# Rotary embedding: most partner rows come by SBUF-to-SBUF transfers from SyncE's queue, not by a TensorE product

## The chip, the cores and the metric
One core of one Trainium2 chip. The metric is the device time of one execution in microseconds; the median of three runs stands for a kernel. A core has TensorE (matmuls), VectorE, ScalarE, GpSimd (POOL) and SyncE, which here only issues transfers. All of them run at once and are ordered by semaphores.

## The reference
Two transformer stacks of two layers each, on 256 tokens with 1024 features in float32; only what matters here:

```python
def apply_rope(x, cos, sin):                 # first stack, heads of 64
    xf = x.reshape(x.shape[:-1] + (HEAD_DIM // 2, 2))
    x0, x1 = xf[..., 0], xf[..., 1]
    return jnp.stack([x0 * cos - x1 * sin, x0 * sin + x1 * cos], axis=-1)
...
        qb = apply_rope(rms_norm(heads(gq, GQA_Q_HEADS), q_gain[l]), cos, sin)
        kb = apply_rope(rms_norm(heads(gk, GQA_KV_HEADS), k_gain[l]), cos, sin)
...
def partial_rope(x, cos, sin):               # second stack, the first 16 of 64
    x1, x2 = x[..., :half], x[..., half:ROPE_DIM]
    r1, r2 = x1 * c - x2 * s, x2 * c + x1 * s
    return jnp.concatenate([r1, r2, x[..., ROPE_DIM:]], axis=-1)
...
    q_c = partial_rope(heads(q_c, N_HEADS_DSA), cos, sin)      # 5 heads
    k_c = partial_rope(k_c[:, :, None, :], cos, sin)[:, :, 0]  # 1, from the compressed keys
    q_i = partial_rope(q_i.reshape(B, S, N_IDX_HEADS, IDX_DIM), cos, sin)
    k_i = partial_rope(rmsnorm(k_i, g_idx_k)[:, :, None, :], cos, sin)[:, :, 0]
```

So in the first stack neighbours (rows 2i and 2i+1 of a head) turn each other, in the second rows i and i+8 of the first 16. Around this stand projections, neighbourhood, grouped-query, forgetting, stick-breaking and sparse attention, and gated feed-forwards.

## The kernel before, in words
Features lie on the 128 partitions, tokens along the free axis, so a chunk of 128 features x 256 tokens holds two heads. Weights come as "pieces" of up to 128 x 2048 (1 MB). SyncE issues them one after another into a ring of four slots: piece n waits until TensorE has begun piece n - 3 (`piece_begun`). ScalarE rounds a piece to its high part `w_hi` (two buffers, L1750), VectorE computes the rest `ring_lo` in the slot (L2267), in halves, and TensorE multiplies high by high, high by low and low by high (L1258 features on the partitions, L1504 tokens on them, L1301 the wide form). Every engine runs its own program in the order in which the host put items into `plan`; there is no scheduler, and VectorE, ScalarE and SyncE never pass over a waiting instruction. An item "inside" another is issued by TensorE among that one's matmuls (`mids`).

A rotation (`rope`) turns 256 tokens of one chunk: TensorE multiplies the chunk with a 128 x 128 matrix of 0, 1 and -1 (`pe_rope`, L1548), which puts each row's partner, with its sign, into a PSUM bank; VectorE multiplies that by the sine table into a scratch (`turned_by`, two halves used in turn), the chunk in place by the cosine table, and adds (`dve_rope`, L2635, L2636, L2638). There are 24: five in each layer of the first stack ("block 1": the key chunk `gk` and four query chunks `gq`), seven in each layer of the second ("block 2": two index-query chunks, two and a half chunks of queries, the index key, the compressed key).

Where they stand. Block 1, layer 0: among attention steps (`att`), which are mixed with gate chunks; a step computes scores (L1572), takes negated maxima (L2668), exponentials (L1989), transposes (L1585) and at times the values' product (L1600). The head norms' factors are spread by L1538 and applied by L2624 (chunks 0 and 1, then 2 and 3, then 4); between them run products for the modulation (L1410), whose weights, `w_mod`, are pieces of the same ring, two at a time (`some(unit, 2)`). Block 1, layer 1: the five are issued among the matmuls of the value product (`tok` of `w_nav`). Block 2: among the chunks of the projection. Two of `w_in`'s chunks lie in a piece; evictions to `arena` scale by the norm (L2496, L2498). `unread` matmuls (L1203) are fillers whose result nobody reads.

SyncE's weight loads are L1188, its first loads L1165 to L1180.

Of the kernel before, what the change touches and what calls it, by code (L numbers as in the profile page):

```python
# [9 lines left out]
ALU = mybir.AluOpType  # L10
# [3 lines left out]
P = 128  # L14
S = 256
D = 1024
KC = D // P
DH = 64
# [37 lines left out]
for _block, _names in (  # L56
        (0, (("ident", P), ("sum_heads", 4 * 32), ("sum_kv", 2 * 32), ("row_sel", 8), ("vec_sel", 64), ("spread", 4 * P))),
        (1, (("rot1", P), ("cos1", S), ("sin1", S), ("na_mask", 2 * S))),
# [10 lines left out]
def constants():  # L69
# [18 lines left out]
    rot = np.zeros((P, P))  # L88
    rot[p[1::2], p[0::2]] = -1
    rot[p[0::2], p[1::2]] = 1  # L90
    put("rot1", rot)
# [5 lines left out]
    put("sin1", np.sin(ang).T[pair])  # L97
# [4 lines left out]
    for h in range(2):  # L102
        for i in range(8):
            a, b = h * DH + i, h * DH + 8 + i
            rot[b, a], rot[a, b] = -1, 1
            cos[a] = cos[b] = np.cos(ang[i])
            sin[a] = sin[b] = np.sin(ang[i])
# [41 lines left out]
class Plan:  # L149

    def __init__(self):
        self.items, self.pieces, self.splits = [], [], []
        self.full, self.taken, self.lin, self.counts = [0] * 8, [0] * 8, 0, {}
        self.in_slot, self.held = [0] * RING, None

# [43 lines left out]
def hybrid_kernel(nc, xt, vec_d, con_d, tables_d, rpb, w, out):  # L199

    with ExitStack() as ctx:
# [130 lines left out]
        setup, silu_c_ready, amp_ready = sem("setup"), sem("silu_c_ready"), sem("amp_ready")  # L332
        x_done, squares, sq_added, rstd_ready = (sem(n) for n in ("x_done", "squares", "squares_added", "rstd_ready"))
# [237 lines left out]

        last_prep, mixed, last_gate = [None], [], [None]
# [57 lines left out]
        def rope(chunks, block, need=(), inside=False, bank=None):  # L630
            return add("rope", block=block, need=need, tb=turned_by if block == 1 else turned_by2, inside=inside,
                       chunks=[(b, a, low, fill(T_BANKS[i % 2] if bank is None else bank) if bank or not inside else linear(), count("rope")) for i, (b, a, low) in enumerate(chunks)])
# [87 lines left out]
        def first_block(l):  # L720
# [18 lines left out]

            def na_pair(i, q0, k0, nk):  # L740
# [37 lines left out]
            if l == 0:  # L778
# [54 lines left out]
                head_spread(hn, 0, 1)  # L833
                some(unit, 2)
# [4 lines left out]
                rope(ropes[:2], 1, need=(hn["spread"][1],))  # L839
# [8 lines left out]
                rope(ropes[2:3], 1, need=(hn["spread"][2],), bank=T_BANKS[1])  # L848
                two_steps(last=False)
                rope(ropes[3:4], 1, need=(hn["spread"][3],))  # L850
                two_steps()
                rope(ropes[4:5], 1, need=(hn["spread"][4],))
# [7 lines left out]
            else:  # L860
# [19 lines left out]
                head_spread(hn, 0, 1)  # L880
                g = attention([dict(na_pair(0, 0, 0, SQ), after=(feats["naq", 0], feats["nak", 0]))])
                att(g)
                run_all(nk[1])
                head_spread(hn, 2, 3)
                vals = values()
                att(g)
                head_spread(hn, 4)
# [4 lines left out]
                among = {4 + 8 * i: rope([r], 1, need=(hn["spread"][i],), inside=True) for i, r in enumerate(ropes)}  # L892
                tok("nav", w["w_nav"][l], 2, SLOT, 512, SQ, nav)
                plan.items[-1]["mids"] = among
                next(vals)
                add("keys_swap", n=plan.counts["rope"] - 4)
# [83 lines left out]
        def second_block(l):  # L980
# [22 lines left out]
            def turned(chunk, bank, *need):  # L1003
                return rope([chunk], 2, need=need, inside=True, bank=T_BANKS[bank])
# [27 lines left out]
            def stick_acc(*hs):  # L1032
                for h in hs:
                    accs.append(fill(T_BANKS[h % 2]))
                    add("stick_acc", h=h, f=accs[-1], n=5 * l + h)

            run_all(chunks(0, fresh=plan.counts["h"], norm=defer()), chunks(1))
            add("y2_pad", after=fc(QI + 1))
            tok(f"vb{l}", w["vb2"][l], 2, 4 * 384, 384, S, vb2, scaled=True, n_out=330)
# [6 lines left out]
            among(t, lambda: {10: [turned((feat2, QI * S, 0), 0, fc(QI))], 18: [turned((feat2, (QI + 1) * S, 0), 1, fc(QI + 1))]})  # L1046
            run_all(t)
            t = chunks(3)
            next(t)
            head_spread(hn, 0, 1)  # L1050
            among(t, lambda: {13: [turned((feat2, 12 * S, 0), 1, fc(12))], 20: [turned((feat2, 13 * S, 0), 0, fc(13))]})
# [5 lines left out]
                              16: [turned((feat2, KX * S, DH), 0, hn["spread"][1])]})  # L1057
            key_turned = plan.counts["rope"]
            add("key_twice", n=key_turned, k=count("key_twice"))
            among(t, lambda: {8: [turned((kc2, 0, 0), 1, kv[0])], 16: [turned((feat2, QX * S, DH), 0, fc(QX))]})  # L1060
            run_all(t)
            among(feat(f"2f{l}", [(0, P, cols(5, 0, P))], [10], S, length=KC * P), lambda: {6: [index(0, 0, 1)], 16: [index(0, 2, 3)]})
            t = chunks(5)
# [100 lines left out]
        def _(sp):  # L1164
# [10 lines left out]

            first_mod(0)
            for p in plan.pieces:
# [5 lines left out]
                for a, n, src in p.srcs:  # L1183
# [4 lines left out]
                    sp.dma_start(dst, src).then_inc(landed[p.slot], 16)  # L1188
            for k in range(4):
# [7 lines left out]
        def _(pe):  # L1197
# [28 lines left out]
            def product(fs, n, groups, fresh=None, need=None, at_col=0, mids={}, more=False, hold=False, odd=None):  # L1226
# [7 lines left out]
                for p, terms in groups:  # L1234
# [6 lines left out]
                    for wpart, part, (at, hi, lo, rows, c), k in order:  # L1241
# [11 lines left out]
                        if at_mm in mids:  # L1253
                            for what, it in mids[at_mm] if isinstance(mids[at_mm], list) else [mids[at_mm]]:
                                dict(sums=pe_sums, spread=pe_spread, att=pe_att, head_spread=pe_head_spread, rope=pe_rope, kvup=pe_kvup,
# [230 lines left out]
            def pe_tok(st):  # L1486
                T, cols, n = st["T"], st["cols"], len(st["pieces"])
                per, at_mm, mids = KC // n, 0, st.get("mids", {})
                for j, p in enumerate(st["pieces"]):
# [3 lines left out]
                    for wt, low in ((w_hi[p.s % 2], False), (ring_lo[p.slot], True)):  # L1493
                        if low:
                            pe.wait_ge(w_lo_ready, 2 * p.s + 2)
                        for t, f in enumerate(st["fs"]):
                            for i in range(per):
                                c, at = j * per + i, i * cols
                                for part in range(1 if low else 2):
                                    if at_mm in mids:  # L1500
                                        pe_rope(mids[at_mm])
                                    at_mm += 1
# [40 lines left out]
            def pe_rope(st):  # L1543
                pe.wait_ge(s_tables, 16 * st["block"])
                taken(*st["need"])
                for buf, at, low, f, _ in st["chunks"]:
                    room(f)
# [697 lines left out]
        def _(dve):  # L2245
# [381 lines left out]
            def dve_rope(st):  # L2627
                b = st["block"]
                dve.wait_ge(s_tables, 16 * b)
                for f in st["need"]:  # L2630
                    taken(f)
# [333 lines left out]
```

## Time and profile before
| | |
|---|---|
| median of 3 runs | 2416.3 us (2415.94 to 2416.79) |
| profiled execution | 2416.34 us |
| its span, first to last instruction | 2414.5 us |
| mean granted TensorE clock | 0.999 of 2.4 GHz |
| TensorE, VectorE, ScalarE, GpSimd busy | 2393.6, 1538.3, 1219.4, 405.0 us |
| transfers | 389.9 MB, 161 GB/s over the span |

A row of a timeline is the start in us from the span's start, the length in us, the engine, the line, the operation, what it writes and reads, its shape and how many were merged; in brackets the idle time before it and what ended it. TensorE's matmul records overlap, so the price of one is read from start to start. SPq is SyncE.

### The profile page before, as it was taken

Reading aid. Unit: us, or ns where it says so; the run is one execution under the profiler, and the core shown is the slowest. Engines: PE = TensorE matmul, PEld = TensorE weight load, DVE = VectorE, ACT = ScalarE, POOL = GpSimd, SP = SyncE. Lnnn points to the kernel's source line nnn. Section 1 sums busy time; section 2 is a strip of 40 time slices with the busy share of each in tenths; the row PEclk is TensorE's granted clock in tenths of the full one; section 3 lists DMA queues with packets and bytes.
Section 4 is the critical chain, followed back from the end, with each engine's and each line's share of the span. In section 5 each row is a group of like instructions: output and inputs, shape, how many; then the busy total and the mean of one; then the engine's idle time right before and its main releaser. Section 6 shows DMA issues by size and latency. Waiting matters only on the chain.

```text
span 2414.5 us, 36498 instructions
## 1 busy us (share of the span) xinstructions
PE 2393.6 (99%) x14216; PEld 2036.5 (84%) x14216; DVE 1538.3 (64%) x2659; ACT 1219.4 (51%) x2268; POOL 405.0 (17%) x388
## 2 busy tenths in 40 slices
PE   8999999999999999999999999999999999999998
PEld 6766689888888877988888899898888889989887
DVE  5335455663455555677677777677767767767775
ACT  4344444322222546565565545665556554566554
POOL 0343322000001335100100100540010010154000
PEclk9999999999999999999999999999999999999999
DMA  6334423453444422455565553355565564436554
GB/s 280 132 114 158 157 88 122 159 169 135 157 165 141 157 89 95 150 192 176 194 212 181 172 184 128 123 193 192 170 208 180 176 195 151 151 112 200 190 175 137
DMA packets 88602, 389.92 MB, mean 161 GB/s; under 512 B 15024, under 2 KB 27600, under 8 KB 58352
## 3 DMA queue, kind: packets, MB, share of 16 engines
q1 hardware_dynamic: 81232, 356.07, 43.4%
q0 software_dynamic: 7200, 31.52, 3.8%
q8 instruction: 114, 1.87, 0.3%
q14 instruction: 56, 0.46, 0.1%
HBM read 386.52 MB, written 1.05 MB: 161 GB/s over the span
## 4 chain that ended last, share of the span: by engine, by line
PE 93%; DVE 3%; ACT 2%; POOL 1%; issue 1%; DMA 0%; DVEq 0%; SPq 0%; POOLq 0%; ACTq 0%
PE ps L1301 42%; PE ps L1258 38%; PE ps L1504 3%; PE ps L1572 2%; PE ps L1585 2%; PE ps L1600 2%; DVE ring_lo L2267 1%; PE ps L1395 1%; ACT logits L1989 1%; ACT w_hi L1750 1%; PE ps L1410 1%; POOL logits L2184 1%; PE ps L1548 1%; DMA x_res<-xt 0%; PE ps L1429 0%
## 5 line engine op out<-in xcount | busy, mean ns | idle before, releaser
L2267 DVE TENSOR_TENSOR ring_lo<-ring,w_hi 128x1024 fp32r<-128x1024 f32 (+4 forms) x708 | 781.8, 1129 | 200.1 <-ACT w_hi L1750 199.0
L1750 ACT ACTIVATE w_hi<-ring 128x1024 fp32r<-128x1024 f32 (+4 forms) x708 | 633.4, 944 | 280.1 <-PE ps L1258 186.7
L1301 PE MATMUL ps<-h_hi,w_hi 128*128 128x512 f32 x2144 | 527.2, 393 | 0.6 <-DVE h_hi L2440 0.3
L1301 PEld LDWEIGHTS ps<-h_hi,w_hi 128*128 128x128 f32 x2144 | 391.3, 188 | 76.6 <-issue 2.5
L1258 PE MATMUL ps<-h_hi,w_hi 128*128 128x256 f32 (+1 forms) x1520 | 410.6, 333 | 2.0 <-ACT arena L1879 1.2
L1258 PE MATMUL ps<-h_lo,w_hi 128*128 128x512 f32 (+1 forms) x976 | 325.5, 351 | 0.0
L1301 PEld LDWEIGHTS ps<-h_hi,ring_lo 128*128 128x128 f32 x2144 | 281.3, 191 | 14.5 <-DVE ring_lo L2267 0.9
L1301 PE MATMUL ps<-h_hi,ring_lo 128*128 128x256 f32 x2144 | 288.2, 282 | 0.0
L1258 PEld LDWEIGHTS ps<-h_hi,w_hi 128*128 128x128 f32 x1520 | 252.3, 190 | 37.6 <-issue 11.2
L1258 PE MATMUL ps<-h_hi,ring_lo 128*128 128x256 f32 (+1 forms) x1248 | 253.3, 338 | 0.3 <-DVE ring_lo L2267 0.3
L2509 DVE TENSOR_TENSOR prob_t<-ps,prob_t 128x256 f32<-128x256 f32 x260 | 109.7, 422 | 196.3 <-ACT prob_t L1902 196.0
L2140 POOL TENSOR_TENSOR logits<-logits 128x256 f32<-128x256 f32 (+1 forms) x65 | 67.6, 1040 | 991.0 <-ACT logits L1771 776.5
L1301 PE MATMUL ps<-hid_both,w_hi 128*128 128x512 f32 x880 | 226.2, 392 | 0.0
L1258 PEld LDWEIGHTS ps<-h_hi,ring_lo 128*128 128x128 f32 x1248 | 200.8, 189 | 28.4 <-issue 2.2
L2184 POOL TENSOR_SCALAR logits<-logits,stat 128x512 f32<-128x512 f32 (+2 forms) x140 | 167.9, 1211 | 261.4 <-DVE stat L2680 261.2
L1902 ACT ACTIVATE prob_t<-ps 128x256 f32<-128x256 f32 x260 | 98.1, 377 | 220.6 <-PE ps L1301 220.3
L1258 PEld LDWEIGHTS ps<-h_lo,w_hi 128*128 128x128 f32 x976 | 182.3, 189 | 23.5 <-DVE h_lo L2440 0.2
L1301 PEld LDWEIGHTS ps<-hid_both,w_hi 128*128 128x128 f32 x880 | 160.8, 188 | 30.9
L1989 ACT ACTIVATE logits<-logits,stat 128x512 f32<-128x512 f32 (+2 forms) x140 | 81.6, 584 | 140.4 <-DVE logits L2668 85.5
L1301 PE MATMUL ps<-hid_both,ring_lo 128*128 128x256 f32 x880 | 133.4, 282 | 0.0
L1301 PEld LDWEIGHTS ps<-hid_both,ring_lo 128*128 128x128 f32 x880 | 122.4, 191 | 5.7
L1928 ACT ACTIVATE prob_t<-prob_t 128x256 f32<-128x256 f32 x110 | 46.0, 418 | 105.3 <-DVE prob_t L2533 93.5
(301 smaller groups left out, 2934.0 us busy)
## 6 DMA issues: line engine op xcount, KB each, us to landing
ring<-w_ffn_in SPq DMA_DIRECT2D x132, 1024.0 KB, 4.9
ring<-w_ffn_out SPq DMA_DIRECT2D x96, 704.0 KB, 4.0
ring<-w_in SPq DMA_DIRECT2D x36, 1024.0 KB, 4.9
ring<-w_w_in SPq DMA_DIRECT2D x26, 1024.0 KB, 5.0
bias_t<-w_mod POOLq DMA_DIRECT2D x24, 1024.0 KB, 5.4
ring<-w_mod SPq DMA_DIRECT2D x16, 1024.0 KB, 6.0
ring<-w_up SPq DMA_DIRECT2D x16, 576.0 KB, 3.8
ring<-w_pab SPq DMA_DIRECT2D x8, 1024.0 KB, 4.9
```

The lines of the kernel that those rows point to most:

```text
L1258: mm = pe.matmul(ps[fs[k].bank][:, at_col:at_col + n], (hi_w if wpart == "hi" else lo_w)[0:rows, at[k]:at[k] + P], hi if part == "hi" else ...
L1301: mm = pe.matmul(ps[f.bank][:, 0:cols], wt[:, at + q * P:at + q * P + P], both[:, 0:cols], start=left[q] == n, stop=left[q] == 1, skip_gro ...
L1504: mm = pe.matmul(ps[f.bank][:, 0:st["n"]], rows, wt[:, at:at + st["n"]], start=c == 0 and part == 0 and not low, stop=c == KC - 1 and low)
L1572: mm = pe.matmul(ps[f.bank][:, s2["at"]:s2["at"] + s2["nk"]], p["q"][a, s2["t"] * P:(s2["t"] + 1) * P], p["k"][a, k0:k0 + s2["nk"]], start ...
L1585: mm = pe.transpose(ps[f.bank][:, c * P:(c + 1) * P], logits[:, o:o + P], ident)
L1750: act.activation(w_hi[q.s % 2][:, h * n:(h + 1) * n], ring[q.slot][:, h * n:(h + 1) * n], ACT.Copy)\
L1902: act.activation(tmp[i][:, S:SQ], ps[f.bank][:, S:SQ], ACT.Copy).then_inc(half_out, 1)
L1989: act.activation(lg, lg, ACT.Exp, scale=-1.0, bias=stat[:, o:o + 1], accum_out=stat[:, 4 + o:5 + o])\
L2140: pool.tensor_tensor(sq_sum[:, o:n], sq_sum[:, o:n], sq[j % 2][:, o:n], ALU.add).then_inc(sq_added, 1)
L2184: pool.tensor_scalar(lg, lg, stat[:, 8 + (a % 2) * 2 + h:9 + (a % 2) * 2 + h], None, ALU.mult)\
L2267: dve.tensor_tensor(ring_lo[q.slot][:, c], ring[q.slot][:, c], plain(w_hi[q.s % 2][:, c]), ALU.subtract)\
L2509: dve.tensor_tensor(tmp[i][:, to:to + S], ps[f.bank][:, 0:S], tmp[i][:, S:SQ], ALU.add).then_inc(psum_taken[f.bank], 1)
```

## The change
Of the 24 rotations 20 lose their product. Instead SyncE copies the chunk's rows, swapped, into the scratch, by transfers from SBUF to SBUF: in block 1 two of 64 rows of every second partition, in block 2 two (or four, for a chunk with two heads) of 8 rows. The sign goes into the sine tables. The four rotations of the index key and of the compressed key keep the product (`product`), with `hroot2` as scratch and a wait for the rotation before. In block 2 the scratch is cleared once, as rows that aren't swapped are multiplied by a sine of 0.

A swap is recorded in `plan.swaps` under a piece's number, and SyncE does it right behind the issue of that piece: two behind the next piece at the time of the call, or more (`later`). SyncE first waits until the chunk is complete, and until the rotation that used the same half of the scratch is done. VectorE's `rope` waits for the landing. In block 1, layer 1, and in block 2 VectorE's rotations take other places in its order.

```diff
+        def swap(chunk, block, need, later=0):
+            buf, at, low = chunk
+            n = count("swap")
+            moves = 2 if block == 1 or low else 4
+            t = dict(buf=buf, at=at, low=low, block=block, need=need, n=n, tb=turned_by if block == 1 else turned_by2,
+                     landed=count(f"swap_landed{n % 2}", 16 * moves))
+            t["before"] = swapped[-2] if n > 2 else None
+            swapped.append(t)
+            plan.swaps.setdefault(len(plan.pieces) + 2 + later, []).append(t)
+            return t
...
+            def swap_rows(t):
+                sp.wait_ge(psum_taken[t["need"].bank], t["need"].taken)
+                if t["before"]:
+                    sp.wait_ge(rope_ready, t["before"]["turned"])
+                src, dst = t["buf"][:, t["at"]:t["at"] + S], t["tb"][:, t["n"] % 2 * S:(t["n"] % 2 + 1) * S]
+                if t["block"] == 1:
+                    for a in range(2):
+                        sp.dma_start(dst[a:P:2, :], src[1 - a:P:2, :]).then_inc(s_swap[t["n"] % 2], 16)
+                    return
+                for h in range(t["low"], P, DH):
+                    for a, b in ((0, 8), (8, 0)):
+                        sp.dma_start(dst[h + a:h + a + 8, :], src[h + b:h + b + 8, :]).then_inc(s_swap[t["n"] % 2], 16)
...
                     sp.dma_start(dst, src).then_inc(landed[p.slot], 16)
+                for t in plan.swaps.get(p.n, ()):
+                    swap_rows(t)
...
# block 1, layer 0
                 head_spread(hn, 0, 1)
+                turned = swaps(0, 1)
...
-                rope(ropes[:2], 1, need=(hn["spread"][1],))
+                rope(*turned)
+                turned = swaps(2, 3, later=2)
                 add("keys_swap", n=1)
...
                 head_spread(hn, 4)
-                rope(ropes[2:3], 1, need=(hn["spread"][2],), bank=T_BANKS[1])
+                rope(turned[0])
+                turned += swaps(4, later=1)
...
# VectorE
             def dve_rope(st):
...
+                dve.wait_ge(s_swap[t["n"] % 2], t["landed"])
+                c, r = t["buf"][low:P, t["at"]:t["at"] + S], t["tb"][low:P, t["n"] % 2 * S:(t["n"] % 2 + 1) * S]
+                link(dve.tensor_tensor(r, r, cn(f"sin{b}")[low:P, :], ALU.mult))
+                link(dve.tensor_tensor(c, c, cn(f"cos{b}")[low:P, :], ALU.mult))
+                dve.tensor_tensor(c, c, r, ALU.add).then_inc(rope_ready, 1)
```

Where the swaps stand in SyncE's order in block 1, layer 0 (`w_w_in` are pieces of the projection, `w_mod` of the modulation, `arena<-arena` the swaps). Before:

```order
L1188 DMA ring<-w_w_in 128x8x128
L1188 DMA ring<-w_mod 128x4x512 x2
L1188 DMA ring<-w_w_in 128x2048
L1188 DMA ring<-w_mod 128x4x512 x2
L1188 DMA ring<-w_w_in 128x2048
L1188 DMA ring<-w_mod 128x4x512 x2
L1188 DMA ring<-w_w_in 128x2048
```

and now:

```order
L1238 DMA ring<-w_w_in 128x8x128
L1220 DMA arena<-arena 64x256 x4
L1238 DMA ring<-w_mod 128x4x512 x2
L1238 DMA ring<-w_w_in 128x2048
L1238 DMA ring<-w_mod 128x4x512 x2
L1238 DMA ring<-w_w_in 128x2048
L1238 DMA ring<-w_mod 128x4x512 x2
L1220 DMA arena<-arena 64x256 x4
L1238 DMA ring<-w_w_in 128x2048
L1220 DMA arena<-arena 64x256 x2
```

Swaps 1 and 2 stand ahead of a pair of modulation pieces, swaps 3 and 4 behind another pair, swap 5 behind the piece after it.

VectorE at the third rotation of the same layer, between the scaling of the last query chunk and the maxima of attention step 17, now:

```order
L2673 SCALAR_TENSOR_TENSOR arena<-arena,q_gain_scaled,ps 128x512
L2683 TENSOR_TENSOR arena<-arena,tables 128x256
L2684 TENSOR_TENSOR arena<-arena,tables 128x256
L2685 TENSOR_TENSOR arena<-arena 128x256
L2316 TENSOR_TENSOR ring_lo_50<-ring,w_hi 128x1024
L2739 RECIPROCAL stat<-stat 128x2
L2727 TENSOR_SCALAR logits,stat<-ps 128x512 x2
```

Here the order is the one of before; only the first operation of the rotation (L2683) reads the scratch instead of a PSUM bank, and waits for a transfer instead of TensorE.

SyncE in a layer of block 2, at the projection's pieces, now:

```order
L1238 DMA ring<-w_vb 128x1536 x2
L1238 DMA ring<-w_in 128x2048
L1224 DMA arena<-arena 8x256 x8
L1238 DMA ring<-w_in 128x2048
L1238 DMA ring<-w_in 128x8x64 x2
L1238 DMA ring<-w_in 128x8x128 x2
L1224 DMA arena<-arena 8x256 x8
L1238 DMA ring<-w_in 128x2048 x2
L1224 DMA arena<-arena 8x256 x2
L1238 DMA ring<-w_in 128x2048
```

The 18 short transfers are all new; the loads around them keep their order.

## Rows read from the trace of the kernel before

**Rows 1.** Page, part 1: busy time, share of the span, instructions of TensorE.
```profile
PE 2393.6 (99%) x14216; PEld 2036.5 (84%) x14216; DVE 1538.3 (64%) x2659; ACT 1219.4 (51%) x2268; POOL 405.0 (17%) x388
```

**Rows 2.** One line's instructions, L1548: duration in ns least/median/most, starts, shapes.
```profile
L1548 PE MATMUL ps<-arena,tables x48: 376/378/483, 204.5 to 2036.3; 128*128 128x256 f32 x40, 64*64 64x256 f32 x8
```

**Rows 3.** Timeline of TensorE, value product of block 1, layer 1.
```profile
854.29 0.39 PE L1504 MATMUL ps<-w_hi,h_lo 128*128 128x512 f32 x1
854.51 0.59 PE L1548 MATMUL ps<-arena,tables 128*128 128x256 f32 x2
...
855.17 0.39 PE L1504 MATMUL ps<-w_hi,h_lo 128*128 128x512 f32 x1
```

**Rows 4.** Timeline of TensorE, third rotation of block 1, layer 0.
```profile
218.58 0.70 PE L1548 MATMUL ps<-arena,tables 128*128 128x256 f32 x2
219.21 1.13 PE L1572 MATMUL ps<-arena 64*128 64x512 f32 x4
```

**Rows 5.** Timeline of TensorE, chunks of the projection in block 2, layer 0.
```profile
1424.85 2.08 PE L1258 MATMUL ps<-h_hi,w_hi 128*128 128x256 f32 x16
...
1427.82 0.70 PE L1538 MATMUL ps<-arena,con 32*128 32x256 f32 x4
1428.44 1.82 PE L1258 MATMUL ps<-h_hi,w_hi 128*128 128x256 f32 x13
...
1432.59 1.12 PE L1258 MATMUL ps<-h_hi,w_hi 128*128 128x256 f32 x8
```

**Rows 6.** Timelines of VectorE, SyncE, ScalarE and TensorE around the second head-norm scaling.
```profile
182.59 0.74 DVE L2624 SCALAR_TENSOR_TENSOR arena<-arena,q_gain_scaled,ps 128x512 f32<-128x512 f32 x1
...
182.90 1.23 SPq L1188 DMA_DIRECT2D ring<-w_mod  x2
...
194.23 2.00 ACT L1750 ACTIVATE w_hi<-ring 128x1024 fp32r<-128x1024 f32 x2 [0.84 <-DMA ring<-w_w_in]
...
196.64 0.49 PE L1258 MATMUL ps<-h_hi,w_hi 128*128 128x512 f32 x1
```

**Rows 7.** Timeline of SyncE at the start; page, part 6: KB, us to landing.
```profile
1.17 0.90 SPq L1167 DMA_DIRECT2D x_res<-xt  x2
...
out<-arena SPq DMA_DIRECT2D x4, 256.0 KB, 2.1
...
con<-consts SPq DMA_DIRECT2D x1, 196.0 KB, 7.8
```

**Rows 8.** SyncE's line L1188 from 217.5 to 217.9; timelines of VectorE and TensorE.
```profile
L1188 SPq DMA_DIRECT2D ring<-w_mod x1: 368/368/368, 217.6 to 217.6; - x1
...
DMA to landing us min/median/max: 7.8/7.8/7.8
...
219.41 0.42 DVE L2635 TENSOR_TENSOR arena<-ps,tables 128x256 f32<-128x256 f32 x1
...
220.54 1.22 DVE L2267 TENSOR_TENSOR ring_lo<-ring,w_hi 128x1024 fp32r<-128x1024 f32 x1
...
222.35 0.69 DVE L2668 TENSOR_SCALAR_CACHE_REDUCE logits<-ps 128x512 f32<-128x512 f32 x1
...
223.61 1.13 PE L1572 MATMUL ps<-arena 64*128 64x512 f32 x4
```

**Rows 9.** Windows at the end: length, busy us (count) by engine, clock, DMA share, GB/s.
```profile
2408.70:2411.00 2.30, 0.05 (x1) 0.00 (x0) 2.21 (x6) 0.00 (x0) 0.00 (x0) 1.00 0.20 76
2411.00:2414.50 3.50, 0.00 (x0) 0.00 (x0) 1.01 (x3) 0.00 (x0) 0.00 (x0) 0.60 0.68 250
```

**Rows 10.** Windows at the start, filler passes (L1203) alone.
```profile
5.00:7.00 2.00, 2.00 (x11) 2.00 (x11) 1.00 1.00 410
...
9.00:10.50 1.50, 1.50 (x14) 1.31 (x12) 1.00 1.03 435
```

**Rows 11.** Timelines of VectorE and ScalarE, block 2, layer 0: an eviction, a split.
```profile
1410.33 0.42 DVE L2498 TENSOR_TENSOR arena<-ps,row 128x256 f32<-128x256 f32 x1 [2.46 <-PE ps L1258]
...
1418.73 2.00 ACT L1750 ACTIVATE w_hi<-ring 128x1024 fp32r<-128x1024 f32 x2
```

More of the change, by code:

```diff
@@ L96, in constants @@
     put("cos1", np.cos(ang).T[pair])
-    put("sin1", np.sin(ang).T[pair])
+    put("sin1", np.sin(ang).T[pair] * np.where(p % 2, 1, -1)[:, None])
     rot = np.zeros((P, P))
@@ L154, in __init__ @@
         self.in_slot, self.held = [0] * RING, None
+        self.swaps = {}
     def add(self, kind, **kw):
@@ L738, in first_block, with swaps @@
             ropes = [(gk, 0, 0)] + [(gq, c * SQ, 0) for c in range(4)]
+            def swaps(*which, later=0):
+                return [swap(ropes[i], 1, hn["spread"][i], later) for i in which]
             def na_pair(i, q0, k0, nk):
@@ L880, in first_block @@
                 head_spread(hn, 0, 1)
+                turned = swaps(0, 1)
                 g = attention([dict(na_pair(0, 0, 0, SQ), after=(feats["naq", 0], feats["nak", 0]))])
@@ L884, in first_block @@
                 head_spread(hn, 2, 3)
+                rope(*turned)
                 vals = values()
                 att(g)
+                turned = swaps(2, 3)
                 head_spread(hn, 4)
@@ L1001, in index, with rows_of @@
                            n=[count("relu") for _ in hs], inside=True)
-            def turned(chunk, bank, *need):
-                return rope([chunk], 2, need=need, inside=True, bank=T_BANKS[bank])
+            def rows_of(c, low=0):
+                return (feat2, c * S, low)
             def among(tile, make):
@@ L1045, in second_block @@
             head_sums(hn)
-            among(t, lambda: {10: [turned((feat2, QI * S, 0), 0, fc(QI))], 18: [turned((feat2, (QI + 1) * S, 0), 1, fc(QI + 1))]})
+            rope(turned_i[0])
+            turned_12 = swap(rows_of(12), 2, fc(12))
+            next(t)
+            rope(turned_i[1])
+            turned_13 = swap(rows_of(13), 2, fc(13))
             run_all(t)
@@ L1541, in pe_head_spread, with pe_product @@
                                 mm.then_inc(psum_full[f.bank], 1)
[L1543 to L1547, printed above, removed]
-                    pe.matmul(ps[f.bank][low:P, 0:S], cn(f"rot{st['block']}")[low:P, low:P], buf[low:P, at:at + S], start=True, stop=True)\
-                        .then_inc(psum_full[f.bank], 1)
+            def pe_product(st):
+                (buf, at, low), f = st["chunk"], st["f"]
+                pe.wait_ge(s_tables, 32)
+                taken(st["need"])
+                room(f)
+                pe.matmul(ps[f.bank][low:P, 0:S], cn("rot2")[low:P, low:P], buf[low:P, at:at + S], start=True, stop=True)\
+                    .then_inc(psum_full[f.bank], 1)
             def pe_att(st):
```

84 lines of the change are left out of this document (48 added, 36 removed).

## The prediction
> **What bounds the kernel now.** I read the page first. TensorE is busy 99% of a 2414.5 us span [rows 1]. So work taken from TensorE's queue comes off the time one for one, unless TensorE then waits; and work added elsewhere costs nothing until TensorE waits for it. Next I looked up the line of the rotation product: 48 pass records are 24 products of two passes each [rows 2]. The timeline of TensorE around the products gives their price, and the timelines of SyncE, VectorE and ScalarE give the slack of what replaces them. The sum is made against the profiled execution, 2416.34 us (the span and 1.8 around it); the median of the runs, 2416.3, is the same number.
>
> **The gain: 20 of the 24 products go.** In the value product of block 1, layer 1, the two passes and the matmul behind them take 854.51 to 855.17, 0.66 us, where a matmul alone took 854.29 to 854.51 [rows 3]: about 0.43 for a product. Five such make 2.15. In layer 0 the first two follow each other and are 0.43 each; the three that stand between attention steps are dearer, 218.58 to 219.21, 0.63 each [rows 4]: 0.86 + 1.9 = 2.75. In block 2 a chunk of 24 matmuls takes 2.97 us (1424.85 to 1427.82) and one with two products 4.15 (1428.44 to 1432.59) [rows 5]: 1.18 for the pair. The pair before it is costed at 0.86, and the chunk that loses one of its two at half of 1.18, 0.59, so a layer gives 2.63 and both 5.26. **Sum of the gain: 2.75 + 2.15 + 5.26 = 10.2 us.**
>
> **What VectorE does instead.** Three operations for a rotation as before, 219.41 to some 220.54, 1.13 us [rows 8]; the first now reads SBUF, as the second always did, so nothing. The new memset in block 2 stands ahead of a split that waits for ScalarE and is one operation; nothing.
>
> **Cost at the first swaps (layer 0).** SyncE reaches swaps 1 and 2 early and waits for the scaling of the head norms, which ends at 183.33 for the second and some 0.65 earlier for the first; the next weight load was issued at 182.90 [rows 6]. Four more issues stand ahead of it now. Issues that wait for nothing follow each other every 0.47 us (two from 1.17 take 0.90) [rows 7]. So swap 1 goes out at 182.7 and 183.2, swap 2 at 183.7 and 184.2, and the load at 184.65, 1.75 us late. Three 1 MB loads then land behind each other, so the third, the gates' piece, is as late. ScalarE waited 0.84 us for that piece and split it from 194.23 to 196.23; TensorE took it up at 196.64 [rows 6]. The cover is 0.4, so TensorE waits **1.35 us**. Bounds: 0 if the split has more cover than I see, 3 if issues take 0.86 us each, as the two from 182.90 did (1.23 for both).
>
> **Cost at swap 3 (layer 0), the term that decides.** The order of SyncE puts swaps 3 and 4 right behind two 1 MB loads of the modulation. The second was issued at 217.6 and landed 7.8 us later, at 225.4 [rows 8]. Transfers of this queue land in the order of issue: a 256 KB store into an idle queue took 2.1 us, but 196 KB of constants took 7.8 us behind 2 MB of loads [rows 7]. So swap 3 lands half a microsecond behind the second load, near 225.9. VectorE wants it where the product's first row stood, at 219.41; it is 6.5 us late. Behind it in VectorE's order stand a low-part split and the maxima of attention step 17, whose second half began at 222.35 and ended at 223.04. TensorE can't write step 18's scores before these have left the banks; it wrote them from 223.61 [rows 8], less the 0.63 of the product 222.98. With the maxima ending at 229.5 it idles 6.5 us, and ScalarE's copy of the turned probabilities, which follows its exponentials of step 17, adds some 0.3: **6.8 us**. Bounds: 1.2 if the swap doesn't queue (issued by 218.5, landed at 220.6), 8 if rows of 1 KB move slower than I think. I take the value near the top, since every row of the queue shows landings in order. After it, swap 4 has landed before it is wanted, and swap 5, which may go once rotation 3 is done, has some 15 us.
>
> **Cost of the clock.** In 2408.70 to 2411.00 TensorE had 0.05 us of work and the granted clock was 1.00; in 2411.00 to 2414.50 it had none and the clock was 0.60 on average [rows 9]. So it falls to 0.5, 1.2 GHz, within some 3 us of the last matmul, and an idle stretch of 6.8 us should do the same. How long it stays low I take from the start of the kernel: of the same filler passes 11 ran in the 2 us from 5.00, and 14 in the 1.5 us from 9.00 [rows 10] (the column reads 1.00 in both; the pace doesn't). They had begun near 3, so some 5.5 us ran at the low pace and lost half of it, 2.7. Bounds 0 and 2.7; I take **2.3**, as TensorE also waits for others in that stretch. The Trainium skill, "TensorE: Matmul & The Clock Gate", Part 1, says that the throttled clock is the default, that sustained activity lifts it and that idling brings it back. By that rule the change pays twice for its one long wait; had the clock no such gate, the sum would be 2.3 us lower. The rows at the end of this trace agree with the rule.
>
> **Costed at nothing.** Block 1, layer 1: VectorE does two rotations (2.3 us) before the maxima of attention step 1 instead of behind them; TensorE needs those banks again only for the value product, and a chunk of 24 matmuls, over 5 us at the 0.22 of [rows 3], stands between. SyncE waits there for each rotation before it swaps into the same buffer, and so holds the next gates' piece some 3 us; the whole value product stands between that piece and its use. Block 2: eight issues of 8-row swaps stand between two 1 MB pieces of the projection. The last four can go when the eviction of 1410.33 ends, at 1410.75, so the piece goes out at 1412.7 and lands some 5 us later at 1417.7, where ScalarE takes it up at 1418.73 [rows 11]: cover 1 us. The next eight wait for rotations 11 and 12 and hold a piece some 3.5 us; another whole piece stands between it and its use. If these covers were gone it would be 1 to 5 us a layer.
>
> **Sum:** 2416.3 - 10.2 + 1.35 + 6.8 + 2.3 = **2416.5 us**, no change.
>
> **The rivals.** (a) *Swap 3 doesn't queue behind the loads*, or half of its wait is covered. For it: it moves 128 rows of 1 KB, and is issued 7 us before the loads are through. Against: [rows 7]. With a wait of 1.2 and no fall of the clock 2416.3 - 10.2 + 1.35 + 1.2 = 2408.7; with half of the wait, 3.4, and no fall, 2410.9. The Trainium skill, "DMA: Bandwidth & Descriptors", Queues, rings and completion order, says that each engine takes descriptors in ring order but that completion isn't in order over the engines; no row read here shows a landing out of order. (b) *The swaps' issues are slow, and the weight loads behind them come late*: slower. In block 2 the piece is in time until eight issues and the waits between put it over 1413.8: from the eviction before, near 1407.9, that is 0.73 us an issue. Above that both layers pay eight times the excess, and the first swaps four times what is over 0.47. At 1.2 us each it is 2 x 3.7 + 2.9 = 10.3, or 2426.8; from 0.93 on it decides against the change. For it: nothing here shows an issue that goes from 8 partitions to 8. Against it: 0.47 and 0.86 are what issues took. (c) *The products' time doesn't come back*, because TensorE, earlier by 10 us in all, waits for softmax or splits instead: half of the gain lost gives 2421.6. Against it: at 99% busy it waits for little anywhere [rows 1].
>
> **How the numbers follow.** The forecast's case, with its terms between their bounds, gets 0.60; (a) 0.25, as it holds the half-covered wait too; (b) 0.09; (c) 0.06. A measurement of this kernel tells about 0.2%, 4.8 us, from no change. (a) is faster by more than that, (b) and (c) are slower, and the forecast's own spread, 2411.5 to 2421, is the same. So faster 0.25, same 0.60, slower 0.15. The range takes in (a) and (c) to their values: 2408.7 to 2421.6.
>
> **What would show it.** The product's line keeps 8 passes of 48. VectorE waits about 6 us for a transfer near 219, and TensorE then idles over 5 us ahead of scores near 223; the granted clock of the stretch behind is under 1.00. ScalarE's wait for the gates' piece near 195 grows from 0.84 to over 2 us. If the clock is full throughout and no wait of TensorE exceeds 2 us, I am wrong towards (a); if SyncE's swaps in block 2 take over 0.7 us each and TensorE waits near 1420, towards (b).

## The result and the profile after

| | before | after |
|---|---|---|
| median | 2416.29 us (2415.94 to 2416.79, 8 runs) | 2422.61 us (2421.54 to 2427.07, 8 runs) |
| ratio | | 1.0030, 95% interval 1.0022 to 1.0039 |
| profiled execution | 2416.34 us, span 2414.5 | 2427.07 us, span 2425.2 |
| mean granted clock | 0.999 | 0.995 |

The change makes the kernel 6.3 us slower, 0.26%. The eight executions of before lie within 0.9 us, those of after within 5.5, and the profiled one is the slowest of them; why will be seen below.

The page of after, the row of busy times (it answers to [rows 1]):

```profile
PE 2390.9 (99%) x14176; PEld 2034.0 (84%) x14176; DVE 1540.8 (64%) x2660; ACT 1219.7 (50%) x2268; POOL 405.3 (17%) x388
```

Forty pass records are gone, as they should be. TensorE's busy time falls by 2.7 us and not by ten: matmuls at half the clock are longer, and count as busy. So the page hides both halves of the story, and I aligned TensorE's matmuls of the two traces one by one. The distance is how much later a matmul starts after the change than before; I looked where it jumps. There are four kinds of places.

**Place A, the first swaps.** SyncE, ScalarE and TensorE of after (start, length, engine, line, what ended the wait), against [rows 6]:

```profile
183.99 2.46 SPq L1220 DMA_DIRECT2D arena<-arena  x4
186.50 1.14 SPq L1238 DMA_DIRECT2D ring<-w_mod  x2
...
198.21 2.00 ACT L1799 ACTIVATE w_hi<-ring 128x1024 fp32r<-128x1024 f32 x2 [3.54 <-DMA ring<-w_w_in]
...
200.36 0.47 PE L1310 MATMUL ps<-h_hi,w_hi 128*128 128x512 f32 x1 [2.18 <-ACT w_hi L1799]
...
201.90 0.63 PE L1310 MATMUL ps<-h_lo,w_hi 128*128 128x512 f32 x1
202.32 0.63 PE L1310 MATMUL ps<-h_hi,w_hi 128*128 128x512 f32 x1
```

Four issues take 183.99 to 186.50, 0.63 us each, and the next load goes out 3.6 us later than before. Of this 1.3 is this execution's own start, where the granted clock was 0.50 from 13.5 to 16.8 us, as it wasn't in the profile of before; 2.3 is the swaps'. ScalarE's wait for the gates' piece grows from 0.84 to 3.54. TensorE waits, and a microsecond later its matmuls start every 0.43 us where 0.23 is normal: the clock is at its lower level. The distance grows by 2.4 us in the wait (1.29 to 3.72) and by 1.55 behind it, to 5.27 at the next scores.

**Place B, swap 3.** SyncE, TensorE and VectorE of after, against [rows 8]:

```profile
221.14 1.23 SPq L1238 DMA_DIRECT2D ring<-w_mod  x2
222.48 2.46 SPq L1220 DMA_DIRECT2D arena<-arena  x4
...
227.08 0.39 PE L1310 MATMUL ps<-h_lo,w_hi 128*128 128x512 f32 x1
...
230.95 0.43 DVE L2683 TENSOR_TENSOR arena<-arena,tables 128x256 f32<-128x256 f32 x1 [7.12 <-DMA arena<-arena]
...
234.86 2.08 PE L1621 MATMUL ps<-arena 64*128 64x512 f32 x4 [7.39 <-DVE logits L2727]
236.87 1.98 PE L1649 MATMUL ps<-prob_t,arena 128*64 128x256 f32 x8
```

The second load landed at 230.43, the rotation began at 230.95. TensorE has one gap of 7.4 us, then the scores take 2.08 us where they took 1.13 in [rows 8]. Windows of after around B (length, busy us and count of PE, PEld, DVE, ACT, POOL; clock; DMA share; GB/s):

```profile
224.00:232.00 8.00, 3.47 (x18) 2.57 (x16) 0.98 (x3) 0.00 (x0) 0.00 (x0) 1.00 0.98 373
232.00:239.00 7.00, 4.14 (x14) 1.53 (x15) 4.95 (x11) 2.31 (x6) 3.63 (x3) 0.52 0.07 26
239.00:244.00 5.00, 5.00 (x28) 3.46 (x26) 3.17 (x9) 2.87 (x7) 3.68 (x3) 1.00 0.01 3
```

The clock falls to 1.2 GHz in the middle of the gap and stays there for 6.8 us. The distance grows from 3.79 to 13.09: 7.5 us in the wait and 1.8 behind it. Of the latter 0.2 is there too where the clock stays up (v3_s34_fillers30 below), so some 1.6 is the clock's.

**Place C, the stick-breaking scores of block 2, in both layers.** VectorE, ScalarE and TensorE of after in layer 0:

```profile
1454.33 0.42 DVE L2683 TENSOR_TENSOR arena<-arena,tables 64x256 f32<-64x256 f32 x1
...
1455.70 2.36 DVE L2316 TENSOR_TENSOR ring_lo<-ring,w_hi 128x1024 fp32r<-128x1024 f32 x2
...
1461.33 0.21 ACT L2118 ACTIVATE small<-small 128x12 f32<-128x12 f32 x1 [1.93 <-DVE small L2810]
...
1465.05 1.99 ACT L1799 ACTIVATE w_hi<-ring 128x1024 fp32r<-128x1024 f32 x2
1466.20 2.36 DVE L2316 TENSOR_TENSOR ring_lo<-ring,w_hi 128x1024 fp32r<-128x1024 f32 x2 [2.33 <-ACT w_hi L1799]
1468.47 1.02 DVE L2875 TENSOR_TENSOR logits<-ps,tables 128x384 f32<-128x384 f32 x2
...
1469.17 0.67 PE L1737 MATMUL ps<-arena 64*128 64x256 f32 x2 [1.31 <-DVE logits L2875]
...
1470.57 3.28 PE L1310 MATMUL ps<-h_hi,w_hi 128*128 128x256 f32 x16
1473.64 1.45 PE L1310 MATMUL ps<-h_hi,ring_lo 128*128 128x256 f32 x8
```

The same before:

```profile
1452.62 0.21 ACT L2069 ACTIVATE small<-small 128x12 f32<-128x12 f32 x1 [1.93 <-DVE small L2751]
...
1457.49 2.36 DVE L2267 TENSOR_TENSOR ring_lo<-ring,w_hi 128x1024 fp32r<-128x1024 f32 x2 [1.46 <-ACT w_hi L1750]
...
1460.51 0.70 PE L1688 MATMUL ps<-arena 64*128 64x256 f32 x2
...
1461.93 2.08 PE L1258 MATMUL ps<-h_hi,w_hi 128*128 128x256 f32 x16
1463.85 1.12 PE L1258 MATMUL ps<-h_hi,ring_lo 128*128 128x256 f32 x8
```

The half chunk's rotation (1.37 us) stands in VectorE's order ahead of two weight splits now. What follows it comes late by as much: ScalarE gets the small values of L2118 1.4 us later against TensorE than before, then works through to its split at 1465.05, for which VectorE waits, and from 1461.33 to TensorE's scores it is 7.84 us, where it was 7.89. So the lateness goes from VectorE through ScalarE and VectorE to TensorE, which waits 1.3 us at its last stick-breaking scores. In this execution sixteen passes behind it take 3.07 us, start to start, where they took 1.92, and the next eight 1.29 for 0.96: 1.5 us more. Layer 1 is the same near 2066 (1.4 and 1.5).

**Place D, the compressed keys' product.** The rotation of the first query chunk (`turned_12`) stands in VectorE's order ahead of the scaling (L2673) that TensorE waits for; before, the scaling came first. It costs 0.5 us a layer:

```profile
1439.14 0.43 DVE L2683 TENSOR_TENSOR arena<-arena,tables 128x256 f32<-128x256 f32 x1
...
1440.41 1.00 DVE L2673 SCALAR_TENSOR_TENSOR arena<-arena,vec,ps 128x256 f32<-128x256 f32 x2
...
1441.46 0.70 PE L1704 MATMUL ps<-arena,kvup 128*128 128x256 f32 x2 [0.30 <-DVE arena L2673]
```

**The sum of the trace.** The gain comes: the distance shrinks by 3.1 us among the attention steps of layer 0, by 1.9 around layer 1's value product and by 2.75 in each layer of the second stack, 10.5 in all. Median: 2416.3 - 10.5 + 4.0 (A) + 9.3 (B) + 2 x 1.4 (C) + 2 x 0.5 (D) = 2422.9, against 2422.6 measured. The profiled execution has 2 x 1.5 more for the clock at C and 1.3 for its own slower start: 2427.2, against 2427.07. So an execution in which the clock falls at C is 1.5 us slower for each. The mean granted clock of the single executions fits: 0.995 in the three of 2424.8 us and more, 0.996 or 0.997 in the five up to 2422.8. Where it fell in them is my reading, as only profiled executions show it.

### The profile page after: what moved, and what is told of

It reads as the page before. It is cut to its first block, busy times and chain, and to the rows that moved or that the text cites. A ratio compares the mean times of both kernels' runs of the same rounds, so it can differ in the third digit from the quotient of the medians.

```text
span 2425.2 us, 36459 instructions
## 1 busy us (share of the span) xinstructions
PE 2390.9 (99%) x14176; PEld 2034.0 (84%) x14176; DVE 1540.8 (64%) x2660; ACT 1219.7 (50%) x2268; POOL 405.3 (17%) x388
## 4 chain that ended last, share of the span: by engine, by line
PE 90%; DVE 4%; ACT 2%; DMA 1%; issue 1%; POOL 1%; SPq 0%; DVEq 0%; ACTq 0%; POOLq 0%
PE ps L1353 42%; PE ps L1310 35%; PE ps L1553 3%; DVE ring_lo L2316 2%; PE ps L1621 2%; PE ps L1649 2%; PE ps L1634 2%; ACT w_hi L1799 1%; PE ps L1447 1%; PE ps L1462 1%; ACT logits L2038 1%; POOL logits L2233 0%; DMA ring<-w_w_in 0%; DMA arena<-w_mod 0%; PE ps L1416 0%
```

## The experiments

Eleven kernels ran, five rounds each, on three chips; the kernel before lay at 2416.29 us beside s1 to s4, 2416.42 beside u and v1, v2, 2416.21 beside v3, w1 and x1. v2_s34_fillers and v3_s34_fillers30 do work whose result nobody reads. Each edit is against the kernel named in its expectation, or against the changed kernel.

| kernel | A | B | C | D | median (range) | ratio, 95% |
|---|---|---|---|---|---|---|
| after | x | x | x | x | 2422.61 (2421.5 to 2427.1) | 1.0030, 1.0022 to 1.0039 |
| s1_early34 | x | | x | x | 2415.28 (2413.2 to 2418.1) | 0.9996, 0.9987 to 1.0004 |
| s2_late12 | | x | x | x | 2419.74 (2418.8 to 2422.0) | 1.0015, 1.0007 to 1.0024 |
| s3_both | | | x | x | 2411.33 (2409.8 to 2413.6) | 0.9981, 0.9972 to 0.9989 |
| s4_q_late | | | | x | 2408.51 (2408.2 to 2408.7) | 0.9968, 0.9955 to 0.9980 |
| u1_q_product | | | product | x | 2409.11 (2408.8 to 2409.9) | 0.9969, 0.9958 to 0.9981 |
| u2_block2_products | | | all products | | 2412.38 (2412.0 to 2413.3) | 0.9983, 0.9974 to 0.9992 |
| v1_s34_back | | x | | x | 2417.25 (2416.6 to 2419.2) | 1.0003, 0.9995 to 1.0012 |
| v2_s34_fillers | | x | | x | 2422.59 (2422.2 to 2424.2) | 1.0026, 1.0016 to 1.0036 |
| v3_s34_fillers30 | | x | | x | 2415.21 (2414.6 to 2416.6) | 0.9996, 0.9987 to 1.0004 |
| w1_s12_back | x | | | x | 2412.23 (2410.9 to 2414.6) | 0.9983, 0.9974 to 0.9992 |
| x1_places | | | | | 2406.60 (2405.9 to 2407.7) | 0.9958, 0.9945 to 0.9972 |

(x: the cost is there. The last column is against the kernel before. "product": the rotation has its product back. A blank at A is no full zero: in the profiles of s2, s3, s4 and x1 the distance still grows by 0.3 to 0.6 us there.)

### Places A and B alone, then both gone

```diff
# s1_early34
-                turned = swaps(2, 3, later=2)
+                turned = swaps(2, 3)
```

> Swaps 3 and 4 of block 1, layer 0, go out two pieces earlier, behind the gates' piece and ahead of the two modulation loads. Theory 1 (swap 3 sat in the queue behind 2 MB): VectorE's wait of 7.12 us and TensorE's of 7.7 near 227 go, and with them the low clock of the 6.8 us behind: 9.1 us less than the changed kernel, some 2413.5. Theory 2 (a swap from SBUF to SBUF takes that long by itself, or VectorE is late for another reason): the wait stays, 2422.

```diff
# s2_late12
-                turned = swaps(0, 1)
+                turned = swaps(0, 1, later=3)
```

> Swaps 1 and 2 of block 1, layer 0, go out three pieces later, behind the gates' piece and not ahead of the modulation loads. Theory 1 (four issues of 0.64 us stand ahead of three loads): ScalarE's wait of 3.54 us near 195 falls back to 0.84, TensorE's 2.18 us go, and the clock stays up there: 3.7 us less than the changed kernel, some 2419. Theory 2 (the rotations' own place on VectorE made the softmax chain late there): ScalarE's wait falls, the time doesn't, 2422.

s3_both has both edits:

> Both moves at once. Theory 1: the two costs lie at places of their own and add up, 12.8 us less than the changed kernel, some 2409.8, which is 6.5 below the kernel before. Theory 2 (one stall covers for the other, the attention chain is the bound): 2413 or more.

Moving swaps 3 and 4 ahead of the two modulation loads takes 7.3 us off, moving swaps 1 and 2 behind the modulation loads and the gates' piece takes 2.9 off, both edits 11.3. In each trace the wait of the place that was edited is gone but for some tenths (0.35 left at A in s2_late12), and the other one stands. The time was 0.7 to 1.8 us above what I expected each time. A part is seen: in s1_early34's profile the four issues at A took 3.37 us, not 2.46, and TensorE waited 2.90 us behind them. The three medians lie in samples 3 to 5 us wide, so a microsecond of them can't be read; their profiled executions show falls of the clock at A and in the second layer's C (s1), at both C (s3), none at C (s2). The eleven times of s3_both alone lie in steps: three at 2409.8 to 2410.0, three at 2411.2 to 2411.3, five from 2412.1 to 2413.6, as none, one and two falls of 1.5 us would have them. So I made the later experiments from a kernel without C.

### Place C

```diff
# s4_q_late, against s3_both
-            rope(turned_q)
             t = chunks(5)
...
             add("index_round")
+            rope(turned_q)
             tok(f"va{l}", w["va2"][l], 2, 4 * 384, 384, S, va2, scaled=True)
```

> As s3, and in block 2 VectorE turns the half chunk of queries only behind the projection's last chunks, before the attention. Theory 1 (its three operations, 1.37 us, moved into VectorE's full stretch of index scores and splits, and made the stick-breaking scores wait, with a fall of the clock behind): the waits near 1467 and 2065 go, 1.3 us and 1.1 of clock a layer, so 4.8 us below s3. Rival (TensorE is 2 us earlier at a stretch that VectorE bounds, whatever is rotated there): s3's time within 1 us.

```diff
# u1_q_product, against s3_both
-            among(t, lambda: {8: [product((kc2, 0, 0), kv[0], 1)]})
-            turned_q = swap(rows_of(QX, DH), 2, fc(QX))
+            among(t, lambda: {8: [product((kc2, 0, 0), kv[0], 1)], 16: [product(rows_of(QX, DH), fc(QX), 0)]})
...
-            rope(turned_q)
```

> The kernel s3_both with the half chunk of queries that shares its chunk with the index weights given back its product on TensorE, at its place of before. My theory: that rotation, moved on VectorE into a stretch where VectorE is the engine behind, makes TensorE wait 1.3 us in each layer of the second stack at the stick-breaking scores, and the clock falls behind it in some executions. Then the waits near 1460 and 2057 go, no clock falls there, and the two passes cost some 0.6 us a layer: 1.2 us above s4_q_late, 2409.7 us. Rival (TensorE comes earlier, by the products that are gone, into a stretch that VectorE sets, whatever the place of this rotation): the waits stay and only the passes are added, 2412.5 us.

Both remove the wait: VectorE's three operations done later (2408.51), or at their place of before with the product (2409.11). The rows of TensorE in s4_q_late at the place of C:

```profile
1453.22 0.64 PE L1310 MATMUL ps<-h_hi,ring_lo 128*128 128x256 f32 x4
1453.79 0.70 PE L1737 MATMUL ps<-arena 64*128 64x256 f32 x2
...
1455.22 1.96 PE L1310 MATMUL ps<-h_hi,w_hi 128*128 128x256 f32 x15
```

No wait, the full pace, and TensorE is 6.7 us earlier there than before the change. So it isn't that TensorE comes early into a stretch which VectorE sets; the rotation's place in VectorE's order is the cause. s4_q_late gains 2.8 us over s3_both, where I had expected 4.8. Aligned with before, it saves both waits of 1.4, but at its new place the rotation costs 0.6 us a layer, at the values' low parts (mended in x1_places): 2.8 - 1.3 = 1.5, close to the 1.3 to 1.4 that s4_q_late lies below the fastest three of s3_both. The rest of its gain over the median fits the clock's falls in the others. Its six executions lie within 0.44 us, those of s3_both within 3.8: with the waits the spread goes too. u1_q_product lies 0.6 us above s4_q_late and not 1.2, as two things partly cancel in the aligned traces: its product costs 0.75 us a layer, and the 0.6 at the values is spared.

### What the second stack gives

```diff
# u2_block2_products, against s4_q_late (a part)
-            rope(turned_i[0])
-            turned_12 = swap(rows_of(12), 2, fc(12))
-            next(t)
-            rope(turned_i[1])
-            turned_13 = swap(rows_of(13), 2, fc(13))
+            among(t, lambda: {10: [product(rows_of(QI), fc(QI), 0)], 18: [product(rows_of(QI + 1), fc(QI + 1), 1)]})
```

> The kernel s4_q_late with all five swaps of each layer of the second stack undone: ten products back at their places of before, no swap there; only the first stack keeps swaps. By the prices of the prediction the first stack gives 2.75 + 2.15 = 4.9 us, so 2411.4 us, and the second stack's share is 2411.4 - 2408.5 = 2.9 us of the 5.3 that its products cost. If swaps in the second stack lost nothing, its share would be 5.3 and this kernel at 2413.8 us.

2412.38: the swaps of the first stack alone give 4.0 us, with their places mended, and those of the second 3.7 to 3.9 more in s4_q_late. The 4.0 are less than the 4.9 of the prediction, though the first stack's passes that are gone are worth 5.35 in the aligned traces. 0.35 is lost at the start of layer 1's value product (see below). 0.45 is lost near attention step 18, in the profile of every kernel whose swaps 3 and 4 go out early: with the product of rotation 3 gone TensorE comes 0.63 us earlier, VectorE's maxima don't, and TensorE waits for them (0.18 in s4_q_late) and at the values' product behind. This is the third rival's mechanism, in small; no run isolates it. And 0.2 us a layer is lost in u2's second stack, whose products are back; why, no run shows.

### Places A and B priced alone

v1_s34_back and w1_s12_back put `later=2` and the early `swaps(0, 1)` back into s4_q_late, one each.

> The kernel s4_q_late with swaps 3 and 4 put back behind the two modulation pieces, nothing else. It prices that one place with every other cost gone: 7.5 us of wait and 1.6 of lower clock behind it, 9.1 us over s4_q_late, 2417.6 us. If what was seen in the trace is partly cover that others would have used, it is 7 us or less, 2415.5.

> The kernel s4_q_late with swaps 1 and 2 put back ahead of the two modulation pieces (behind piece 19), nothing else. It prices that place with every other cost gone. From the trace of the changed kernel: four issues of 0.64 us hold the piece of the gates, TensorE waits 2.5 us near 197 and pays 1.25 for the lower clock behind it: 3.75 us over s4_q_late, 2412.3 us. By the prediction's 1.35 it would be 2409.9 us.

B costs 2417.25 - 2408.51 = 8.7 us, A 2412.23 - 2408.51 = 3.7. The trace of after had 9.3 and 4.0 against the kernel before. But s4_q_late itself loses 0.45 at the place of B and 0.3 at that of A, and against it they are 8.9 and 3.7, as measured within 0.2. That is why the difference of two traces, aligned matmul by matmul, may be trusted here.

### The wait and the clock, apart

```diff
# v2_s34_fillers, against v1_s34_back (v3_s34_fillers30: 30 for 64)
                     inside = g["last"]
+                    if inside["i"] == 18:
+                        inside["fillers"] = 64
...
+                for _ in range(st.get("fillers", 0)):
+                    pe.matmul(ps[V_BANK][:, S:S + P], ones[:, :], ones[:, :], start=True, stop=True)
                 if at < len(steps):
                     scores(at)
```

> The kernel v1_s34_back with 64 matmuls of 128 columns that nobody reads ahead of the scores of attention step 18, where TensorE waits: some 6.8 us of work at the 0.107 us of one, inside the wait of 7.4. It adds work that nothing needs. My theory: the wait stays as long, but the clock doesn't fall, so the time is 1.6 to 2.1 us below v1_s34_back, 2415.8 us. Rival: what follows the wait is slow for another reason than TensorE's idling; then it is no faster than v1_s34_back, 2417.6 us, or slower by what the fillers overrun.

> The kernel v1_s34_back with 30 matmuls that nobody reads ahead of the scores of attention step 18, in place of the 64 of v2_s34_fillers, which were 128 passes and took 14.45 us, twice the wait of 7.2. Thirty are 60 passes at 0.113 us, 6.8 us, inside the wait. My theory: the scores begin where they began in v1_s34_back, and the 1.65 us that the lower clock cost behind them (2.01 and 1.72 where 1.06 and 1.02 would do) are gone: 2415.6 us against 2417.25. Rival: the passes behind the wait are slow for another reason, and the time stays at 2417.25 us.

TensorE of v1_s34_back:

```profile
221.87 0.39 PE L1310 MATMUL ps<-h_lo,w_hi 128*128 128x512 f32 x1
229.10 2.08 PE L1621 MATMUL ps<-arena 64*128 64x512 f32 x4 [6.84 <-DVE logits L2727]
231.11 1.79 PE L1649 MATMUL ps<-prob_t,arena 128*64 128x256 f32 x8
232.83 1.09 PE L1634 MATMUL ps<-con,logits 128*128 128x128 f32 x8
```

and of v3_s34_fillers30:

```profile
222.55 6.86 PE L1657 MATMUL ps<-ones 128*128 128x128 f32 x60
229.71 1.13 PE L1623 MATMUL ps<-arena 64*128 64x512 f32 x4 [0.30 <-DVE logits L2731]
230.98 1.08 PE L1651 MATMUL ps<-prob_t,arena 128*64 128x256 f32 x8
231.99 1.09 PE L1636 MATMUL ps<-con,logits 128*128 128x128 f32 x8
```

The sixty-four were a miss of my own: I took the 0.107 us of a pass for that of a matmul, which has two passes in float32, so they ran 14.45 us and over the end of the wait (2422.59). Thirty fit, end 0.3 us before VectorE does, and the scores behind them have their 1.13 us again. Kernel v3_s34_fillers30 does 6.9 us more work on TensorE than v1_s34_back and is 2.0 us faster: 2415.21 (2414.6 to 2416.6) against 2417.25 (2416.6 to 2419.2), or 1.8 when each is set against the kernel before on its own chip (the intervals of those ratios overlap, the ranges of the runs don't). In the two aligned traces B is 1.3 us cheaper with the thirty. So of B's 8.7 us some 7 are the wait and 1.3 to 2 the clock. The rival, that the passes behind the wait are slow for another reason, falls.

### The version that beats both

```diff
# x1_places, against s4_q_late
-            rope(turned_12)
             head_spread(hn, 0, 1)
+            rope(turned_12)
             next(t)
-            rope(turned_13)
             run_all(t)
+            rope(turned_13)
...
-            rope(turned_q)
             tok(f"va{l}", w["va2"][l], 2, 4 * 384, 384, S, va2, scaled=True)
             stick_acc(1, 0)
+            rope(turned_q)
```

> The kernel s4_q_late with three of VectorE's rotations in each layer of the second stack in other places of its order: rotations 12 and 13 (and 17 and 18) of the two query chunks behind the scaling of the compressed keys and behind the next chunk, instead of ahead; the half chunk's behind the first two stick-breaking products instead of ahead of the values' splits. In s4_q_late TensorE waits 0.22 us at the compressed keys' product and 0.35 at the values' low parts, and the aligned starts lose 0.3 and 0.4 there in each layer. If VectorE's place alone is the cause these go: 1.4 us less, 2407.1 us. If the waits only move on to the next VectorE-fed product, it stays at 2408.5 us.

2406.60 us, 9.6 below the kernel before on the same chip, and 1.9 below s4_q_late where I had expected 1.4. The waits at C and D are gone, and the second stack's layers gain 2.75 us each. In the first stack some tenths are left: the 0.45 near step 18, and at A 0.55 in this profile, where the gates' piece, with the swaps issued right behind it, took 9.8 us to land and not 9.0, and ScalarE waited 1.66 us for it and not 0.84. The three rotations were moved together, so D by itself is read from traces and no run prices it alone.

## Why the prediction was wrong

Forecast 2416.5, no change; measured 2422.6, 6.1 us more and outside of the range (its top was 2421.6), and slower by 0.26% where slower had a chance of 0.15.

- **The gain, 10.2 us: right.** The aligned trace has 10.5, with 2.75 for a layer of the second stack (2.63 predicted); x1_places keeps 9.6 of it in the median.
- **Swap 3, 6.8 us, and the clock behind it, 2.3: the mechanism right, 9.1 predicted for 9.3** in the trace and 8.7 as a difference of medians. That the number fits so closely is partly luck, as two misses cancel: the wait was 7.5, as the second load took 8.4 us to land and not 7.8, and the clock cost 1.6. Rival (a), that the swap doesn't queue, is out: the load ahead landed at 230.43, and VectorE, which waited for the swap alone, began at 230.95. The Trainium skill, "DMA: Bandwidth & Descriptors", Queues, rings and completion order, has each DMA engine take its ring's descriptors in order; by that rule the place in SyncE's order sets when a swap lands, and s1_early34, which changes only that place, agrees.
- **The first swaps, 1.35 us: the wrong size, 3.7.** The step that failed is "issues that wait for nothing follow each other every 0.47 us". That was the pace of two whole-row loads; the swaps take 0.63 each, 64 rows of every second partition. So the first load is 2.3 us late, not 1.75, and it took 0.5 us longer to land; the gates' piece lands 2.7 us late, and the extra wait is 2.4. I had allowed up to 3. What I had not thought of is the clock: I gave it a price only behind the wait of 6.8 us, and it fell behind this one as well, for 1.3 to 1.55 us.
- **"Costed at nothing", block 2: wrong, and the larger half of the miss.** I had costed two things there, the issues and the pieces behind them, and they are free as I said: an issue took 0.70 on average (1417.37 to 1423.01 for eight; rival (b) began at 0.73), and ScalarE has the next piece when it wants it (it waits for TensorE, not for a transfer):

```profile
1417.37 5.59 SPq L1224 DMA_DIRECT2D arena<-arena  x8
1423.01 6.16 SPq L1238 DMA_DIRECT2D ring<-w_in  x5
1423.69 2.01 ACT L1799 ACTIVATE w_hi<-ring 128x1024 fp32r<-128x1024 f32 x2 [2.10 <-PE ps L1553]
```

  But VectorE's rotations moved too, and the step that failed is "three operations for a rotation as before ... so nothing": their number is the same, their place isn't. The half chunk's stands 1.4 us of work ahead of a chain from VectorE over ScalarE back to VectorE that had nothing to spare: 1.4 us a layer, 1.5 more where the clock falls, and 0.5 at the compressed keys. Together 3.8 us without the clock. The order of VectorE of before and after, which I read at swap 3, would have shown it here, and the trace of before shows how busy VectorE is around the scores:

```profile
1461.90:1463.90 2.00, 2.00 (x19) 2.00 (x18) 1.94 (x7) 1.32 (x3) 0.00 (x0) 1.00 0.39 57
```

  (a window of before just behind the place of the wait: VectorE busy 1.94 of 2.00 us, against 64% over the span). This share alone doesn't prove it: just ahead of the scores VectorE itself idled 1.46 us for ScalarE's split (1457.49, above). It is the chain that has no slack.
- **Rival (c)**, TensorE earlier and waiting for others: what was lost at C and D is over a third of the gain (3.8 of 10.2) where I had priced a half. Its mechanism is refuted at C by s4_q_late: the wait came from an operation put ahead, not from TensorE's being early. It is seen only near step 18, for 0.45 us.
- **Block 1, layer 1**, costed at nothing, cost 0.35 us. SyncE's eight transfers ahead of a weight load made nothing wait. But VectorE's two rotations ahead of the maxima put ScalarE's exponentials and the split behind them 2.3 us later, and the value product begins 0.35 us late.

The terms that were missing are 2.4 to 2.65 us (A) and 3.8 (C and D): with them 2416.5 becomes 2422.7 to 2423.0, where 2422.6 was measured.

## What to carry over

A single share of busy time says nothing of a stretch: where an edit moves an operation within an engine's order, count what is put ahead of what at the new place, and follow what comes behind it through the other engines to the one that bounds the time. A short transfer in the queue of the big loads costs not its size but its place: ask what was issued just ahead of it, and what load now stands behind it. And a place is best priced on a kernel without the others: B was 7.3 us beside A and C, and 8.7 alone. A wide spread of the runs is a hint that a wait is left.

## What the runs showed of the hardware that I had not expected

**The granted clock falls behind short waits.** At C TensorE waited 1.31 us in one piece; the windows of after around it (columns as above):

```profile
1461.00:1468.00 7.00, 6.86 (x57) 6.38 (x55) 4.61 (x13) 5.59 (x9) 0.00 (x0) 1.00 0.36 115
1468.00:1472.00 4.00, 2.83 (x17) 2.68 (x18) 3.93 (x13) 2.23 (x5) 0.00 (x0) 0.87 0.11 18
...
1470.50:1473.60 3.10, 3.10 (x18) 3.10 (x18) 2.80 (x11) 2.39 (x6) 0.00 (x0) 0.58 0.49 145
```

TensorE works without a pause from 1470.5 on, 3.4 us of it at 1.2 GHz, and loses 1.5 us: as much again as the wait. In the four profiled kernels that have this wait it stands in eight places, and behind five of them the clock fell: both of after and of s3_both, one of s1_early34, and none of s2_late12:

```profile
1464.32 0.67 PE L1737 MATMUL ps<-arena 64*128 64x256 f32 x2 [1.31 <-DVE logits L2875]
...
1465.72 2.08 PE L1310 MATMUL ps<-h_hi,w_hi 128*128 128x256 f32 x16
```

The Trainium skill, "TensorE: Matmul & The Clock Gate", Part 1, says that an idle window brings the lower clock back and that the window runs free of the kernel. The trace agrees as to B, where the clock stayed low for 6.8 us; and a window that runs free of the kernel may punish the same wait in one execution and not in the next, as at C. Why a wait of 1.3 us with work on both sides is enough for it, no run here shows. The spreads fit: w1_s12_back, whose one long wait is of 2.1 us, ranges over 3.7 us, s4_q_late over 0.44, the kernel before over 0.9 to 1.5. But not every fall is the change's: four of the thirteen profiles (after, u2, v3, x1) have one at 13.0 to 13.5 us, in the kernel's start, which put them 0.5 to 1.3 us behind. x1_places ranges over 1.8 us, and its profiled execution, the slowest, has it.

**Issues of short transfers aren't cheap.** A transfer of 64 rows of every second partition holds SyncE for 0.46 to 0.67 us in after (at A one every 0.63), one of 8 rows for 0.62 to 0.78. Two loads of 1 MB took 1.23 together [rows 6], and the first loads 0.45 each [rows 7].

**Work that nobody reads can shorten the time**: thirty matmuls inside a wait that was there anyway gave 1.3 to 2 us. That is worth less than to have no wait: s4_q_late, which has neither, is 6.7 us below.
